# Banded attention and the memory's output: TensorE products of constants ahead of its waits, and attention outputs that share one PSUM bank

## What is computed

```python
def mlstm_out(h, oa):
    h = rms_norm(h.transpose(0, 2, 1, 3), a_norm_g.reshape(A_HEADS, A_HEAD_DIM))
    return (h.reshape(h.shape[0], h.shape[1], A_WIDTH) * jax.nn.sigmoid(oa)).astype(oa.dtype)

def one_block(args):                       # banded_window_attention, block of 128 queries
    s_win = jnp.einsum('bqhgd,bkhd->bhgqk', qn, kn).astype(jnp.float32) * scale
    s_win = jnp.where(valid_n, s_win, -jnp.inf)
    s_ctx = jnp.einsum('bqhgd,bchd->bhgqc', qn, k_ctx).astype(jnp.float32) * scale
    p = jax.nn.softmax(jnp.concatenate([s_win, s_ctx, s_sink], axis=-1), axis=-1).astype(v.dtype)
    o = (jnp.einsum('bhgqk,bkhd->bqhgd', p[..., :nw], vn)
         + jnp.einsum('bhgqc,bchd->bqhgd', p[..., nw:nw + n_ctx], v_ctx))
```

## Time and profile before

| | us |
|---|---|
| median of 3 runs | 3971.15 |
| lowest, highest | 3954.02, 3973.99 |
| profiled execution, span from first to last instruction | 3963.2 |
| TensorE busy | 3764.1 |
| VectorE busy | 2080.1 |
| ScalarE busy | 1388.4 |

### The profile page before, as it was taken

One profiled execution on the slowest core, in us unless ns is written; L12 is line 12 of the kernel. 1 busy time (PEld: TensorE's weight loads), 2 busy tenths in 40 slices (PEclk: granted clock), 3 DMA queues, 4 the chain that ended last, 5 costly groups with the idle time before them and its releaser, 6 DMA issues.

```text
span 3963.2 us, 44512 instructions
## 1 busy us (share of the span) xinstructions
PE 3764.1 (95%) x18460; PEld 3114.7 (79%) x18460; DVE 2080.1 (52%) x3673; ACT 1388.4 (35%) x2106; POOL 86.1 (2%) x164
## 2 busy tenths in 40 slices
PE   8998989999999999999999978999999999799998
PEld 5985489999986678888887856888788877577886
DVE  5936757644456452333337476433633375765335
ACT  4434533212256442322226533222322256333222
POOL 0100001111000000000000000000000000000000
PEclk9998999999999999999999968999999999789999
DMA  6410014433320122232222201222222222012222
GB/s 222 153 47 1 1 43 131 126 125 128 104 69 27 43 85 98 97 111 99 98 96 80 85 6 43 91 96 99 85 100 96 96 83 82 22 33 85 97 100 80
DMA packets 92885, 333.33 MB, mean 84 GB/s; under 512 B 11365, under 2 KB 11533, under 8 KB 92429
## 3 DMA queue, kind: packets, MB, share of 16 engines
q1 hardware_dynamic: 77040, 278.10, 20.9%
q0 software_dynamic: 12800, 41.95, 3.5%
q10 hardware_dynamic: 2844, 10.44, 0.7%
HBM read 328.35 MB, written 2.10 MB: 83 GB/s over the span
## 4 chain that ended last, share of the span: by engine, by line
PE 88%; DVE 6%; ACT 5%; issue 1%; DMA 0%; DVEq 0%; ACTq 0%; SPq 0%
PE PS L511 74%; PE PS L1078 2%; PE PS L513 2%; PE PS L1094 1%; PE PS L1063 1%; PE PS L1066 1%; PE PS L1424 1%; PE PS L944 0%; PE PS L2394 0%; PE PS L716 0%; PE PS L1395 0%; PE PS L2023 0%; DVE H_r L680 0%; ACT ring_hi L371 0%; DVE XH L879 0%
## 5 line engine op out<-in xcount | busy, mean ns | idle before, releaser
L511 PE MATMUL PS<-arena_r,ring_hi 128*128 128x512 f32 (+1 forms) x6224 | 2104.8, 376 | 76.8 <-DVE H_r L680 69.7
L511 PE MATMUL PS<-arena_r,ring_r 128*128 128x512 f32 (+1 forms) x4752 | 1780.0, 375 | 0.0
L511 PEld LDWEIGHTS PS<-arena_r,ring_hi 128*128 128x128 f32 x6224 | 1167.2, 189 | 260.2 <-DVE H_r L680 60.8
L511 PE MATMUL PS<-H_r,ring_hi 128*128 128x512 f32 (+1 forms) x3280 | 1229.7, 375 | 0.0
L511 PEld LDWEIGHTS PS<-arena_r,ring_r 128*128 128x128 f32 x4752 | 896.5, 189 | 131.4
L380 DVE TENSOR_TENSOR ring_r<-ring,ring_hi 128x1024 fp32r<-128x1024 f32 x514 | 626.9, 1221 | 659.8 <-ACT ring_hi L371 659.3
L371 ACT ACTIVATE ring_hi<-ring 128x1024 fp32r<-128x1024 f32 x514 | 541.4, 1055 | 871.4 <-DMA ring<-weights_dram 863.6
L511 PEld LDWEIGHTS PS<-H_r,ring_hi 128*128 128x128 f32 x3280 | 621.9, 190 | 95.5 <-issue 3.1
L1654 ACT ACTIVATE arena<-PS 128x512 f32<-128x512 f32 x88 | 52.6, 598 | 528.6 <-PE PS L511 528.6
L1232 DVE SCALAR_TENSOR_TENSOR XH<-PS,mods,XH 128x256 f32<-128x256 f32 (+1 forms) x144 | 68.5, 524 | 235.3 <-PE PS L511 235.3
L342 DVE CAST arena_r<-arena 128x512 fp32r<-128x512 f32 (+1 forms) x184 | 74.1, 403 | 199.4 <-ACT arena L1278 196.4
(11 more groups left out here) (372 smaller groups left out, 3104.2 us busy)
## 6 DMA issues: line engine op xcount, KB each, us to landing
ring<-weights_dram SPq DMA_DIRECT2D x526, 512.0 KB, 3.3
rstd<-ada_later_dram POOLq DMA_DIRECT2D x54, 256.0 KB, 2.9
mean<-ada_later_dram POOLq DMA_DIRECT2D x53, 256.0 KB, 3.0
ada_extra<-ada_later_dram POOLq DMA_DIRECT2D x53, 256.0 KB, 3.0
XH<-xT_dram ACTq DMA_DIRECT2D x1, 3072.0 KB, 19.5
ring<-weights_dram ACTq DMA_DIRECT2D x4, 512.0 KB, 4.0
out_dram<-XH SPq DMA_DIRECT2D x8, 256.0 KB, 2.0
con<-second_dram ACTq DMA_DIRECT2D x1, 1536.0 KB
```

What stands on the lines that cost most here:

```text
L511: ins = pe.matmul(PS[:, o.bank, 0:hi - lo], w[:, 0, :], x, **flags)
```

## The change

A helper `keep_busy(pe, n, dst)` issues n products of the ones matrix with the first columns of `con` into a part of PSUM that nobody reads; with 256 columns each is a plain float32 product of 128 rows and 128 columns. It is called in three places: 6 products at the start of `mlstm_out_pe` into bank 0; 4 ahead of each head's wait for `mo_ht` into bank 2h, which the head's transposes then overwrite; and one in steps 2 to 19 of the banded attention, between the step's outputs and the wait for `at_n`, into bank 7 (`filled=20`). To free bank 7, outputs of groups with 64 columns in use all go to bank 6, even groups to partitions 0 to 63 and odd ones to 64 to 127. `attn_c` keeps banks 6 and 7 and has no filler.

```diff
+        def keep_busy(pe, n, dst):
+            for _ in range(n):
+                pe.matmul(dst, C("ones"), con[:, 0:dst.shape[-1]], start=True, stop=True)
-        def attention(groups, scale, p_at, pt_at, by_diagonal):
+        def attention(groups, scale, p_at, pt_at, by_diagonal, filled=0):
+            def out_of(gi):
+                m = groups[gi]["m"]
+                return PS[m * (gi % 2):m * (gi % 2) + m, 6, :] if m == 64 else PS[:, 6 + gi % 2, :]
-                            ins = pe.matmul(PS[0:g["m"], 6 + gi % 2, :], g["v"](kts[t]), turned[gi % 2][:, t, :],
+                            ins = pe.matmul(out_of(gi), g["v"](kts[t]), turned[gi % 2][:, t, :],
                                             start=(t == 0), stop=(t == len(kts) - 1))
                         kts = key_tiles(g)
+                        if i < filled:
+                            keep_busy(pe, 1, PS[:, 7, 0:256])
                         pe.wait_ge(at_n.sem, at_n.at("pe", u))
-                        g["put"](PS[0:g["m"], 6 + gi % 2, :].rearrange("p (h q) -> p h q", h=4)).then_inc(at_oc.sem, 1)
+                        g["put"](out_of(gi).rearrange("p (h q) -> p h q", h=4)).then_inc(at_oc.sem, 1)
         def mlstm_out_pe(pe):
+            keep_busy(pe, 6, PS[:, 0, 0:256])
             for h in range(4):
                 if h == 2:
                     pe.wait_ge(dup_copied.sem, 1)
+                keep_busy(pe, 4, PS[:, 2 * h, 0:256])
                 pe.wait_ge(mo_ht.sem, h + 1)
-        attn_b = attention(b_groups(), 64 ** -0.5, 0, 18464, False)
+        attn_b = attention(b_groups(), 64 ** -0.5, 0, 18464, False, filled=20)
```

## The result

The changed kernel takes 3986.5 us (median of 14 runs, 3972.4 to 3988.9) where the kernel before takes 3971.6 (14 runs, 3954.0 to 3977.7). The ratio is 1.0027, with a 95% interval of 1.0018 to 1.0036: slower by some 11 us. The forecast was -0.4 us. The changed kernel's times fall into two groups: six runs from 3972.4 to 3975.8 us, eight from 3986.5 to 3988.9. The profiled execution is of the upper group (3986.5 us).

A forecast was written before the change was run, and what follows sets the result against it. TensorE was taken as the bound where the attention's clock is low. Attention starting 7.0 us late at 370.5, step 24 at 423.6 against 423.98: -0.4 us from 3971.15 gives 3970.8 us, range 3956 to 3987.

The forecast's parts named there:

- the rise after four steps: Banded attention: after falling near its start, the clock returns to 2.4 GHz after four steps of 2.7 us, 10.8 us.
- The term for steps 16 to 24: Banded attention: these steps, fillers included, take 20.5 us, without the clock's fall at 404.4.
- long lower level: Rival, attention: fillers don't raise the clock before step 12 and cost 0.9 us each; +11 us, 3982 us; chance 0.2.
- the case that I held likeliest: Attention: one short dip of the clock, then 2.4 GHz; -0.4 us in all; chance 0.45.
- The memory's output: Stage ahead of the attention: its fillers make the attention start 7.0 us late, bounds 5.5 and 8 us.
- The fall at the attention's start: Between the last transposes and first filler, 4.3 us with three score products alone: the clock falls near 373 us.
- The held clock: Rival: fillers of the memory's output keep 2.4 GHz through the attention's start; -5.1 us, 3966 us; chance 0.25.
- Fillers without effect: Rival, attention: the clock runs as without fillers, with the second fall after 404; +19 us, 3990 us; chance 0.1.
- The shared bank: 64-row outputs in halves of bank 6: taken as costing nothing, bounds nothing and 9 us.
- The base: Kernel before: attention start to step 24 takes 60.5 us (363.48 to 423.98), its clock's course taken as given.
- behind it nothing changes: After step 24: latent groups stay at 1.00 without fillers, and each later stage starts when the one ahead has ended.

The follow-up runs named there:

- h2: The changed kernel itself, nothing altered, executed once more with its own profile: 3977.1 us.
- f3: Changed kernel without the memory's output's fillers, with 4 fillers added ahead of the attention's third score product, its 18 kept: 3961.1 us, 0.9973 of the kernel before.
- e2: Changed kernel with the fillers of the memory's output alone, none in the attention: 3982.6 us, 1.0022 of the kernel before.
- g3: Changed kernel with 4 more fillers ahead of the attention's third score product: 3963.1 us, 0.9978 of the kernel before.
- f2: Changed kernel with fillers moved into TensorE's waits around the memory's output and attention start, without the 18 step fillers: 3973.6 us, 1.0006 of the kernel before.
- e4: Changed kernel with fillers moved into TensorE's waits around the memory's output and attention start, the 18 step fillers kept: 3957.2 us, 0.9965 of the kernel before.
- e1: Changed kernel without any filler, only the shared bank 6 kept: 3973.9 us, 1.0007 of the kernel before.
- h1: The changed kernel itself, nothing altered, executed once more with its own profile: 3987.0 us.

## Why the prediction was wrong, point by point

**The step that failed** is the length of the lower level in the attention. I took "the rise after four steps: nearer to the doubling", some 10 us. In six profiled executions it was 41 us five times and 30.7 once, with TensorE busy throughout. Step 24, which I had at 53.1 us after step 0 (423.6 less 370.5), was at 67.8. These 14.7 us are the miss: the forecast's -0.4, plus 14.7, less the 1.5 us by which the memory's output was shorter than forecast, plus the 0.65 from ahead of it, are 13.5 us, and by that much step 24 starts later than before (437.44 and 423.98). The term for steps 16 to 24, 20.5 us, was right (20.7). The trace of before had said it: a rise took 27 us there with TensorE busy throughout the second half, and I set that row aside for an analogy with the doubling. The rival "long lower level" had this mechanism and, up to step 12, the right sum: 36.3 us after step 0, measured 35.5. Its steps of 2.75 and 4.65 us were 2.73 and 4.63. It let the level rise at step 12, where it rose at step 14, and so had step 24 3.2 us too early after step 0 (64.6 for 67.8). That it ended at +11 us (3982), and the ratio gives 11 us too, is in part luck: the profile has 13.5 us up to step 24 and 7.8 behind it, and the profile of h2 has 10.3 and 1.5. By its own terms it should have been the likeliest case, and had 0.2. That the median lies just inside the range is owed to this rival, whose time set the upper end, and not to the case that I held likeliest. The Trainium skill (TensorE: Matmul & The Clock Gate, Part 1) has sustained activity release the throttle; 40.80 us of 40.80 at 0.50, busy by the profile, disagree, as the trace before did, and the four fillers of f3, followed by a rise within 3.4 us, agree.

**The memory's output**: 7.0 us forecast, 5.5 measured, at the lower of my bounds and for the reason given with it: the level rose at 355.0, 1.5 us earlier, and a head took 2.38 us and not 2.55. In the profiles of h2 and e2, where the level rose 6.2 us into the stage, it was the forecast 7.0 us (19.3 us for the stage). That these fillers are on the path was right, and e2 shows it.

**The fall at the attention's start** was right (372.1; I had near 373), and so was its cause, as g3 shows by filling that stretch: there it doesn't fall.

**The held clock** as a rival gave step 24 at 48.4 us after the start (418.9 less 370.5). In g3, where the level does hold, it is 49.7: the terms of filler and step were right to 1.3 us. Nearly all of that is in the nine steps 7 to 15: the sum has 17.1 us for them, where the prediction's own 1.5 and 2.5 us a step give 18.5, and g3 took 18.3. Its condition was not met by this change.

**Fillers without effect** is refuted: f2 against e4, 18 fillers more and 16 us less. In the changed kernel itself, though, its 18 bought nothing that can be seen (e2 without them 1.0022, with them 1.0027).

**The shared bank**: nothing, as taken; e1 leaves at most 6 us. The Trainium skill's statement (PSUM — Partial Sum Buffer, on bank collisions) that different quadrants of a bank may be accessed at once agrees with it: the output beside a copy in e1 took its usual 1.07 us.

**The base**: I took the kernel before's course of the clock as fixed. e1 shows 61.3 us low for the same work, so 60.5 us to step 24 was no firm base; and 7.8 us of the profile's difference lie in later stages, for which I had "behind it nothing changes". From the projection's first product to the end, untouched by any of these edits, the profiled executions took from 3454.8 us (before) to 3463.5 (h1), so a single profile's span can't settle a few us. What makes a later stage's level fall for longer after a stage 1500 us earlier has shifted is open; the time of its start has moved against the course of the clock, and no run here fixes that.

## What to carry to other kernels

Products of constants are worth something only where TensorE otherwise waits: find those waits in the timeline, size the fillers to them (here 4 products in 1.85 us), and look first at the join of two stages, where the first products stand alone. A level once lost need not come back because the profile shows the engine busy (here it took 41 us); a filler at the lower level costs twice and may buy nothing. One profile shows one course of the clock, so compare several executions, and prefer the version whose times stand in one group.

## What the hardware showed that I had not expected

TensorE, busy 40.80 of 40.80 us by the profile, nearly a third of it with the 12 fillers, stays at 1.2 GHz; yet with eight filler records in a row at the attention's start the level is up within 3.4 us (f3). The two lengths 41.0 and 30.7 us recur to 0.1 us between executions of two kernels. And four plain products, 1.7 us of work that nobody reads, move the whole by 10 us in f3 and by some 20 in g3 (1.0027 to 0.9978).
